# Two transformer blocks on one core: stick attention and out projection in one program, embedding between its blocks, residual adds on VectorE, late square sums on TensorE

## The reference, cut to what matters

```
proj = rms_norm(h, g_mix_pre) @ w_in          # u (512), q, k, v (512 each, 8 heads of 64)
y_pool = pool_mixer(u, w_pool, pool_scale)    # trailing means, 4 groups
o_sb   = stick_breaking_attention(q, k, v)
y_sb   = rms_norm(o_sb per head) * g_sb
h = h + rms_norm(concat(y_pool, y_sb) @ w_out, g_mix_post)
m = square(relu(rms_norm(h, g_mlp_pre) @ w_up)) @ w_down      # hidden width 4096
h = h + rms_norm(m, g_mlp_post)
h = h + sigmoid(h @ w_ple_gate) * rms_norm(p @ w_ple_proj, g_ple)   # p has width 256
```

## Time and profile before

| | |
|---|---|
| median of 3 runs | 3318.76 us |
| profiled execution | 3321.36 us (span 3319.6 us) |
| PE busy | 3026.9 us, 91% of the span |
| DVE busy | 1604.1 us, 48% |
| POOL busy | 1103.5 us, 33% |
| ACT busy | 786.7 us, 24% |
| mean granted TensorE clock | 0.945 of 2.4 GHz |

### The profile page before, as it was taken

How to read it: one execution, slowest core, us unless ns; L and a number is a source line. 1 busy time by engine, 2 the same in 40 slices (tenths; PEclk the granted TensorE clock), 3 DMA queues, 4 the chain that set the end, 5 groups by cost and what they waited for, 6 DMA issues and landing times. The chain is left out here.

```text
span 3319.6 us, 34583 instructions
## 1 busy us (share of the span) xinstructions
PE 3026.9 (91%) x13308; PEld 2397.8 (72%) x13308; DVE 1604.1 (48%) x1535; ACT 786.7 (24%) x1036; POOL 1103.5 (33%) x506
## 2 busy tenths in 40 slices
PE   6999959799999997789999696799888999999997
PEld 5876547588888886568888564677676788888885
DVE  3649844655555555861130466645434443333335
ACT  2148821311111113230011244133202211111111
POOL 2320023444444444533443311310233434334341
PEclk9999989899999998889999698889999999999998
DMA  2121031122222222221123330200231111111111
GB/s 102 50 57 26 20 133 32 51 89 83 88 85 80 86 70 90 84 91 50 45 87 114 96 77 26 64 13 14 102 120 38 45 51 47 48 51 44 51 51 57
DMA packets 67286, 216.33 MB, mean 65 GB/s; under 512 B 8704, under 2 KB 15104, under 8 KB 66304
## 3 DMA queue, kind: packets, MB, share of 16 engines
q1 hardware_dynamic: 62224, 196.28, 18.8%
q10 hardware_dynamic: 4976, 18.88, 1.4%
HBM read 170.49 MB, written 22.54 MB: 58 GB/s over the span
## 5 line engine op out<-in xcount | busy, mean ns | idle before, releaser
L267 POOL TENSOR_TENSOR w_hi<-w_raw,inv_count 128x1024 fp32r<-128x1024 f32 x203 | 389.8, 1920 | 1771.4 <-PE ps L292 1206.3
L270 POOL TENSOR_TENSOR w_lo<-w_raw,w_hi 128x1024 fp32r<-128x1024 f32 x203 | 537.2, 2646 | 15.9
L292 PE MATMUL ps<-x_hi,w_hi 128*128 128x512 f32 x1280 | 400.9, 395 | 30.8 <-POOL w_lo L270 10.5
L292 PE MATMUL ps<-x_lo,w_hi 128*128 128x512 f32 x1280 | 399.3, 394 | 0.0
L292 PE MATMUL ps<-x_hi,w_lo 128*128 128x512 f32 x1280 | 399.0, 393 | 0.0
L292 PEld LDWEIGHTS ps<-x_hi,w_hi 128*128 128x128 f32 x1280 | 243.8, 191 | 84.4 <-issue 21.1
L292 PEld LDWEIGHTS ps<-x_lo,w_hi 128*128 128x128 f32 x1280 | 244.0, 191 | 51.3
L292 PEld LDWEIGHTS ps<-x_hi,w_lo 128*128 128x128 f32 x1280 | 243.6, 190 | 51.4
L292 PE MATMUL ps<-hidden_hi,w_hi 128*128 128x512 f32 x832 | 257.4, 391 | 4.3 <-DVE mix L1454 4.3
L292 PE MATMUL ps<-y_hi,w_hi 128*128 128x512 f32 x800 | 247.5, 391 | 12.1 <-PEq L2480 9.0
L292 PE MATMUL ps<-hidden_lo,w_hi 128*128 128x512 f32 x832 | 257.0, 390 | 0.0
(11 more groups left out here) (369 smaller groups left out, 4783.8 us busy)
## 6 DMA issues: line engine op xcount, KB each, us to landing
w_raw<-wall SPq DMA_DIRECT2D x221, 512.0 KB, 3.6
ada_raw<-wada SPq DMA_DIRECT2D x48, 512.0 KB, 4.3
gates_scratch<-gate_out ACTq DMA_DIRECT2D x16, 512.0 KB, 2.6
residual<-x_t SPq DMA_DIRECT2D x8, 512.0 KB, 8.5
emb_scratch<-emb_out ACTq DMA_DIRECT2D x8, 512.0 KB, 2.7
residual<-x_t SPq DMA_DIRECT2D x2, 2048.0 KB, 10.7
embedding<-emb_scratch SPq DMA_DIRECT2D x2, 2048.0 KB, 12.1
residual_scratch<-residual SPq DMA_DIRECT2D x1, 4096.0 KB, 12.1
```

Source lines behind the costliest of these rows:

```text
L267: nc.gpsimd.tensor_tensor(w_hi[:, slot, :], w_raw[:, slot, :], one.to_broadcast([P, S]), ALU.mult).then_inc(w_split, 1)
L270: nc.gpsimd.tensor_tensor(w_lo[:, slot, :], w_raw[:, slot, :], w_hi[:, slot, :].bitcast(F32), ALU.subtract).then_inc(w_split, 1)
L292: last = nc.tensor.matmul(ps[:, banks + c, :], lhs, x[:, k0 + k, c * HALF:(c + 1) * HALF], start=(left == nk * 3 - 1), stop=(left == 0))
```

## The change

**Order of weights.** The ten blocks 17 to 26 become: out 0, out 1, embedding, out 2, out 3, embedding, out 4 to 7. The first program now also splits block 18, so both first out blocks are split before the attention begins.

**Stick attention joins the program of out1 to in2.** Inside its last head pair ScalarE also casts the four pool tiles to `y_hi` and squares head tiles 0 to 2 (one such 128x1024 operation after every second step), VectorE takes their remainders at the last four steps (`pool_low`). Buffers move: `y_hi` to slots 24 to 31, `y_lo` to two pieces, `mix` to 32 to 39, apart from the down sums.

**out1.** The four pool rows of the first two blocks are multiplied first, with the head sums between them, then their head rows; the embedding follows, four tiles after out 0 and 1 and four after out 3. Its tiles are copied out of PSUM on ScalarE (was VectorE). p is loaded at the start of out1, x after the heads are split.

**Residual halves.** `residual_half` does scale, add and remainder of three successive tiles in turn, all on VectorE, for both halves. `next_two` issues the sum of the other half after step 2 (was 6 or 7; for in2 3, was 5), and ScalarE computes its root between the tiles of half 0.

**mlp1.** SP loads blocks 30 and 31 at once, a 4 KB piece of `cols2` (`norm_mix`) and the condition row after them. The ada product is eight tiles per loop turn in six turns (was six in seven and a rest): two after `hidden`, ahead of `add_down`, and two after it. The gain for in2 is formed at the end of the loop. The squares of half 0 are added on VectorE, those of half 1 by one TensorE matmul each (`square_stat`, into bank 6), five in the tail and three in `next_two` of the gate.

**gate and in2.** The first weight load stands ahead of the embedding's and of the residual's store; the waits for the embedding's stores are on ScalarE in mlp1. The table load of in2 stands earlier.

The diff, cut to its core:

```diff
+OUT1_ROWS = (17, 18, 89, 19, 20, 90, 21, 22, 23, 24)
@@ first program, POOL @@
-            for b in range(18):
+            for b in range(19):
@@ stick_scalar, in the loop over steps i @@
+            n = i - last_of_pair(2) - 2
+            if 0 <= n < 14 and n % 2 == 0:
+                if n < 8:
+                    pool_high(n // 2)
+                else:
+                    head_square(n // 2 - 4)
@@ stick_vector @@
+            if i >= NS - 1:
+                pool_low(i - NS + 1)
@@ out1_tensor @@
+        head_stat(0)
+        for u in range(2):
+            pe.wait_ge(w_split, (GO + u) * 2 + 2)
+            for n in range(2):
+                for g in range(2 * n, 2 * n + 2):
+                    if u == 0:
+                        pe.wait_ge(*pool_lo.at(g - 3))
+                    out1_tiles((GO + u) % 2, u, (g,), (0, 1), first=g == 0)
+                if u == 0 or n == 0:
+                    head_stat(1 + 2 * u + n)
...
+        pe.wait_ge(*p_lo_done.at(2))
+        use_block(pe, GO + 2, (GO + 2) % 2, 2, 4, p_hi, p_lo, 0, 2, 0, 2)
+        out1_whole(GO + 3, 6)
+        out1_whole(GO + 4, 7)
+        use_block(pe, GO + 5, (GO + 5) % 2, 2, 4, p_hi, p_lo, 0, 8, 0, 2)
+        out1_whole(GO + 6, 12)
@@ residual halves, both on VectorE @@
+    def residual_half(dve, src, gain, c, low_gain=None, between=None):
+        for k in range(10):
+            if k < 8:
+                residual_scaled(dve, src, gain, k, c)
+            if between is not None:
+                between(k)
+            if 1 <= k < 9:
+                residual_sum(dve, src, k - 1, c)
+            if k >= 2:
+                residual_low(dve, k - 2, c, low_gain)
@@ mlp1_sync @@
-        sp.wait_ge(*tile_tmp.at(16))
-        sp.dma_start(c_act[:, 0, :], c_row).then_inc(loaded.sem, 16)
-        sp.wait_ge(*stat_full.at(1))
...
         load_next(first)
         load_next(first + 1)
+        sp.wait_ge(*stat_full.at(0))
+        sp.dma_start(norm_mix[:, :], cols2[:, COLS2["norm_mix"]:COLS2["norm_mix"] + 8]).then_inc(mod_in.sem, 16)
+        sp.wait_ge(*tile_tmp.at(16))
+        sp.dma_start(c_act[:, 0, :], c_row).then_inc(loaded.sem, 16)
@@ mlp1_pool @@
-        split_blocks(pool, GM + 1, GM + 2)
-        for k in range(8):
-            residual_add(pool, mix, k)
-        split_blocks(pool, GM + 2, GM + 64)
-        for n in range(1, 12):
-            square_sum(pool, n)
+        split_blocks(pool, GM + 1, GM + 64)
@@ mlp1 loop, VectorE @@
                 hidden(i * 8 + (GM + 10 + 4 * n), 1 - n, i * 4 + (6 + 2 * n), 2 - 2 * n)
+                multiply_ada(i, range(4 * n, 4 * n + 2))
                 add_down(i * 8 + (GM + 12 + 4 * n), i * 12 + (12 + 6 * n), 2 * n)
-                multiply_ada(i + 1, range(3 * n, 3 * n + 3))
+                multiply_ada(i, range(4 * n + 2, 4 * n + 4))
@@ tail of mlp1, TensorE, half 1 @@
-                if c == 1 and q == 3:
+                if c == 1 and q == 1:
...
+                    half_stat(pe, 0, 4).then_inc(stat_full.sem, 1)
+                if c == 1 and q >= 3:
+                    square_stat(pe, 8 + q - 3)
```

More of the change, by code:

```diff
@@ L41 @@
     W_TOTAL += _n
+OUT1_ROWS = (17, 18, 89, 19, 20, 90, 21, 22, 23, 24)
 def wall_row(b):
-    if W_AT["ple"] <= b < W_AT["out1"]:
-        return b + 72
-    return b - 2 if W_AT["out1"] <= b < W_AT["gate"] else b
+    if W_AT["ple"] <= b < W_AT["mlp1"]:
+        return OUT1_ROWS[b - W_AT["ple"]]
+    return b - 2 if W_AT["mlp1"] <= b < W_AT["gate"] else b
 COLS1, COLS2 = {}, {}
@@ L247, in load @@
             sp.dma_start(w_raw[:, b[1], :], at_row(wall, row)).then_inc(w_landed[b[1]], 16)
-        for low, high in ((0, W_AT["out1"]), (W_AT["out1"], W_AT["gate"]), (W_AT["gate"], W_TOTAL)):
+        for low, high in ((0, W_AT["mlp1"]), (W_AT["mlp1"], W_AT["gate"]), (W_AT["gate"], W_TOTAL)):
             b0, b1 = max(first, low), min(last, high)
             pairs = max(0, b1 - b0) // 2
-            if pairs > 1:
+            if pairs > 1 and low:
                 with sp.Fori(0, pairs) as i:
@@ L1010, in _program, with stick_sync, stick_gpsimd @@
-    o_square = slots("stick_o_square", 12, 4)
+    def stick_sync(sp):
+        for p in range(1, 4):
+            if p == 1:
+                sp.wait_ge(*q_zeroed.at(2))
+            else:
+                sp.wait_ge(*z_full.at(last_of_pair(p - 2)))
+                sp.wait_ge(*q_spread.at(64 * p))
+            spread_q(sp, p)
+            if p == 1:
+                load_blocks(sp, GO + 3, GO + 4)
+        sp.wait_ge(*q_spread.at(256))
+    def stick_gpsimd(pool):
+        for t in q_wide[1]:
+            nc.gpsimd.memset(t[:, :, :, :].bitcast(F32), 0.0).then_inc(q_zeroed.sem, 1)
@@ L1011, in _program, with out1_block @@
+    emb_out = slots("emb_out", 4, 4)
     o_rstd = slots("stick_o_rstd", 4, 4)
     e_msq = temp("emb_mean_square", 4, 1)
-    GP, GO = W_AT["ple"], W_AT["out1"]
+    OUT1_JOBS = [("mix", 0), ("mix", 1)] + [("emb", k) for k in range(4)] + [("mix", 2), ("mix", 3)] \
+        + [("emb", k) for k in range(4, 8)] + [("mix", 4), ("mix", 5)]
+    GM = W_AT["mlp1"]
+    def out1_block(job):
+        kind, k = OUT1_JOBS[job]
+        return GO + ((2, 5)[k // 4] if kind == "emb" else k + (0, 1, 2)[k // 2])
@@ L1015, in mix_half, with wait_out1 @@
+    def wait_out1(eng, job):
+        kind, k = OUT1_JOBS[job]
+        if kind == "mix":
+            wait_tile(eng, out1_block(job), 1, 0, 0)
+        else:
+            wait_tile(eng, out1_block(job), 4, k % 4, 3 * (k // 4))
     def mix_half(dve, u, c, n):
@@ new lines, in out1_scalar @@
+        waiting = None
+        for job, (kind, k) in enumerate(OUT1_JOBS):
+            square(job)
+            if waiting is not None:
+                store(waiting)
+                waiting = None
+            if kind == "emb":
+                emb_copy(job)
+                waiting = job
+            if job == 12:
+                act.wait_ge(*stat_full.at(5))
+                nc.scalar.activation(rstd[:, 0, :], pair(2), ACT.Ln, bias=eps[:, 0:1], scale=-1.0 / D
+                                     ).then_inc(rstd_ready.sem, 1)
+                act.wait_ge(*rstd_ready.at(9))
+                nc.scalar.activation(rstd[:, 0, :], rstd[:, 0, :], ACT.Exp, scale=-0.5).then_inc(rstd_ready.sem, 1)
+                act.wait_ge(*rstd_ready.at(10))
+                act.dma_start(emb_dram[8, :, :], rstd[:, 0, :]).then_inc(emb_stored[0].sem, 16)
@@ L1170, in out1_vector @@
+            if kind == "mix":
+                dve.wait_ge(*pair_free.at(job))
+                nc.vector.tensor_copy(mix[:, k, :], pair(job % 2)).then_inc(pair_free.sem, 1)
         dve.wait_ge(*loaded.at(32))
@@ L1299, in mlp1_scalar @@
         load_exp_ln()
-        act.wait_ge(*emb_stored[0].at(48))
+        for n in range(4):
+            act.wait_ge(*emb_stored[n].at(48 if n == 0 else 32))
         act.wait_ge(*stat_full.at(-1))
@@ L1509, in gate_pool @@
     def gate_pool(pool):
-        split_blocks(pool, GG, GG + 1)
-        for n in range(12, 14):
-            with before(MLP1):
-                square_sum(pool, n)
-        split_blocks(pool, GG + 1, GG + 2)
-        for n in range(14, 16):
-            with before(MLP1):
-                square_sum(pool, n)
-        for k in range(8):
-            residual_add(pool, acc, k)
-        split_blocks(pool, GG + 2, GG + 9)
+        split_blocks(pool, GG, GI + 1)
     def gate_square(act, k, c=None):
```

738 lines of the change are left out of this document (360 added, 378 removed).

## The result

The changed kernel takes 3240.01 us (median of 4 runs, 3236.85 to 3241.66), the kernel before 3318.11 us (median of 4 runs too, of which one took 10203.46): ratio 0.9764, 95% interval 0.9745 to 0.9783, so 2.4% faster. Forecast were 3235 us, 3213 to 3262. The profiled execution took 3241.66 us, span 3238.6, against 3321.36 and 3319.6: 81.0 us of span are gone.

A forecast was written before the change was run, and what follows sets the result against it. TensorE sets the pace nearly everywhere, with its stalls at four boundary stretches the ground to win. Savings of 42.3 + 12.4 + 28.6 + 2.0 = 85.3 us from 3321.36 give 3236.1, stated as 3235 us, range 3213 to 3262.

The forecast's parts named there:

- Out1: From the attention's end to out1's end: 122.2 us against 167.0, so 44.8 us saved.
- Entry of mlp1: mlp1's start: TensorE resumes 5.4 us earlier, block 30's earlier load saves 7.0 us; 12.4 us in all.
- part 1: Stick attention to out1's end: net 42.3 us saved; 38 us if the new waits let the clock fall.
- the first rival: Less comes back, in attention, embedding tiles, cold new waits and mlp1's end: 3255 us, chance 0.22.
- seven extra ScalarE operations: Inside the attention: 1.04 us each, extra need 6.7 us, taken as 2.5 us longer; ends 0 and 6.7.
- split long before: At out1's start: blocks 17 and 18 are split well ahead, so the 3.87 us head-square wait goes; no cost charged.
- The loop: mlp1's loop: VectorE's two multiplications ahead of add_down leave a margin of 0.6 us; cost 0.
- more comes back: Shorter waits keep 2.4 GHz, 3 us each at blocks 29, 30 and 93; no attention loss: 3220 us, chance 0.14.
- End of mlp1, entry of gate: mlp1's tail to block 93: TensorE there at 1349.2 instead of 1377.8, 28.6 us saved; ends 22 and 32.
- first remainder near 1309.8, a wait of 2.2: Gate's entry: VectorE's first residual remainder near 1309.8 us, TensorE waiting 2.2 us instead of 7.52.
- Entry of in2: in2's start: gain no longer waits for cols, half 1 starts 1.2 us earlier; 2 us saved, ends 0 and 4.

The follow-up runs named there:

- the edit of the kernel before: Kernel before the change, with out1's first weight block asked for ahead of the two transfers of x: 3302.82 us, ratio 0.9955.
- The late load: Changed kernel, with the loads of mlp1's blocks 30 and 31 held until the second half sum is there: 3241.8 us, ratio 0.9775.
- The earlier banks: Changed kernel, with gate's first half tiles in banks whose last reader is two VectorE operations further back: 3234.42 us, ratio 0.9749.

## Why the prediction was right, and where it was not

**The large terms held, by their mechanisms.** Out1: 122.2 us laid out, 122.58 measured. No stall at the head sums or at the first embedding tile (0.5 us had been put there); the two new waits are 1.53 us, inside 1.2 to 1.6, and no other stands between embedding tiles. The 21.17 us were the weight in SyncE's queue, which the edit of the kernel before shows alone for 13.4 of them. Entry of mlp1: 5.4 and 7.0 us forecast, block 29 waits 3.82 instead of 4.03 and starts 5.2 us sooner against out1's end, block 30 waits 1.21 instead of 8.18. The late load brought that wait back, 6.98 us longer.

**The clock in part 1.** A wait of 1.53 us was followed by a pair of 0.73 us and then by pairs of 0.62, both times and in all ten profiles that have these waits, like the 1.06 us of the earlier trace rows: the high level of 2.4 GHz was kept. The 4 us that the first rival charged for new waits that start cold are in no run. The part gave 41.7 us, not 38. That figure came from my stretching a page: the Trainium skill (TensorE: Matmul & The Clock Gate, the section on oscillation) tells of a kernel whose waits for transfers, about 3 to 5 us each, let every next piece start at the low clock, and does not say this of waits of 1.5 us. Where this kernel waits 3.8 us, ahead of block 29, the trace agrees with the page: pairs of about 1.05 us follow, at once or within 2 us, in the changed kernel and in all its variants.

**Wrong in its cause: "seven extra ScalarE operations ... I take 2.5 us longer".** The attention ended 3.05 us later, and the number looks confirmed. It is not: the seven cost about 0.7 us, the rest is the start. (Seven times 1.04 is also 7.3, not the 6.7 of the sum.) The step that failed is one clause of part 1, that block 18 is "split long before", costed at nothing without asking what stands behind that split. It stands ahead of a meeting of all engines, and POOL finishes it at 216.97 us; TensorE's wait there went from 1.19 to 4.47 us. That the total came out is luck: one term was too large and one missing.

**The loop: 2.8 us not forecast as likeliest.** All of it is in block 30 itself. From its start to the first matmul of the next down block it was 13.81 us before (636.53 to 650.34) and is 11.02 now (582.74 to 593.76): before, after the wait of 8.18 us, the first pair took 1.19 us and those behind it 1.05, up to 642.61 us, then 0.62; now they take 0.73 and 0.62. With the late load the slow pairs end sooner, after 4.4 us instead of 6.1, and the price is 2.0. This was the 3 us term of the rival "more comes back".

**End of mlp1, entry of gate: 28.6 forecast, 25.8 measured.** The forecast "first remainder near 1309.8, a wait of 2.2" counted VectorE and left out what else TensorE needs: a free pair. The remainder was in fact there 48.2 us after the last up block, earlier than the 50.1 forecast. The add that frees it is queued behind two residual operations that block 92's split stretches to 2.38 and 2.82 us, so TensorE waited 5.33 us. The earlier banks gave 1.5 to 2.1 us of that. The tail ahead of it was also mis-sized, 50.5 us instead of 47.9: behind each of five sums the first matmul of a half tile takes 0.64 us to the next start (1244.19 to 1244.83) instead of 0.23, 2 us in all, which the forecast left out. The waits for the modulation products, 4.33 and 8.30 us, were worth 12.8 us as waits and 5.5 by the clock, as the run that restores them shows.

**Entry of in2: 2.0 forecast, nothing measured.** The 0.8 us of the table lie in gate's loop; the entry itself went from 41.44 to 41.54 us. The gain's early start brought TensorE's first wait from 7.11 to 6.85 us only: two scales that took 0.75 and 0.74 us before now take 3.41 together, where one microsecond more had been put. And ScalarE's root of half 1 stands between two tiles of half 0. That costs TensorE 1.47 us of wait and was left out of the sum for this entry, though the same move was priced at mlp1; undoing it gave 1.35.

So the total, 5 us off, rests on two misses of 2.8 us that cancel, and on one right size with a wrong cause; what is left of the miss is in2 and the part behind it. One slip helped as well: 3236.1 less 2.6 is 3233.5, not 3235.

## What to carry to other kernels

When a step is moved forward and costed at nothing, look for the next meeting of engines behind it: whatever stands ahead of one is on everybody's path. For each operation that TensorE starts with, list all that it waits for, the free bank as well as the operand, and read each from the queue of the engine that gives it. Price a removed wait with its restart: here 12.8 us of waits came with 5.5 us of low clock. And read the clock from all pairs behind a wait, not from the first.

## What the runs showed of the hardware that was not expected

- The same program, with the same wait of 3.82 us ahead of block 29, resumed once at the low clock (first pair 1.22 us) and once at the high one (0.73 us), only to fall low 1.5 us later. In the changed kernel and its eleven variants and repeats slow pairs follow that wait (3.8 to 4.0 us) each time, and the work up to block 30 takes 14.2 to 15.8 us. After the 2.49 us ahead of block 101 five of the fourteen profiles show no slow pair, nine do.
- From block 101 to the end it is 1826.4 to 1833.3 us for the same instructions, and 6.7 us lie between two profiles of one program. A difference of some 7 us between two single executions of this kernel shows nothing; the distance from block 30 to the half sum repeats within 0.02 us (657.28 to 657.30).
- Beside a split on POOL a VectorE cast of 128x512 took 1.89 us instead of 0.43 and a remainder of 128x256 1.99 instead of 0.42 (kernel with block 18's split moved).
